# Two fused transformer blocks on one core: the first phase in another order (sums of squares in pairs, embedding chunks between the modulation chunks, stores between the loads)

## The chip, the core and the metric

One core of a Trainium2 chip runs the whole program in one launch. The metric is the device time of an execution in microseconds. 2467.18 us is the median of three runs of the kernel before (2466.94 to 2468.97). The profile is of a single further execution.

## What is computed

A residual block with adaptive modulation, a recurrent branch and latent attention, followed by a second block with sparse attention, spatial gating and a gated embedding; 512 positions, width 2048, float32. What the first phase makes is this part:

```python
def rms_norm(x, gain=None):
    xf = x.astype(jnp.float32)
    y = xf * lax.rsqrt(jnp.mean(xf * xf, axis=-1, keepdims=True) + EPS)
...
    c_act = jax.nn.silu(c)
    mod = c_act @ w_ada[l] + b_ada[l]
    shift, scale, gate = jnp.split(mod, 3, axis=-1)
    h = rms_norm(x) * (1.0 + scale[:, None, :]) + shift[:, None, :]
    proj = h @ w_in[l]
    xr, gr, qc, kvc, kr, ga = jnp.split(proj, split_points(IN_SPLITS), axis=-1)
...
        x = x + jax.nn.sigmoid(x @ w_ple_gate[l]) * (p[l] @ w_ple[l])
```

The last product, `p @ w_ple`, needs nothing but inputs. The kernel makes it in the first phase and parks it in DRAM until the end.

## The kernel before

**Weights.** All weights come as a stream of chunks of 128 x 1024 float32 (512 KB), in the order of the list `PLAN`; a chunk lies in one of twelve slots (`raw`, `rawx`) while the first phase lasts, and SyncE (SP) issues its load when the chunk twelve places before it has been used. To multiply in float32 precision, a chunk is split: ScalarE (ACT) writes the rounded upper half `whi` (L1146), GpSimd (POOL) the difference `wlo` (L2496), and TensorE (PE) does three matmuls per 128 x 128 block: `whi` with the activations' upper half (L535), `whi` with their lower half (L536), `wlo` with the upper half (L538). PE can begin with `whi` and stops at the third matmul if `wlo` is not there.

**The first phase.** The list `OPENING` sets the order of the work on PE, ACT and VectorE (DVE), each of which walks through it in its own program:

- `ple` m: one of four chunks of the embedding product, 4 blocks of 6 matmuls, 24 in all. Block n writes PSUM bank n % 6, and must wait until ACT has copied out the block that was there (L1208) into a staging tile `stg`, from where SP stores it (`pls`, L2616).
- `xsum`: the sum over the features of x squared, by matmuls with a tile of ones (L597). ACT makes the squares (L1179); then comes the root on ACT (L1221) and the reciprocal on DVE (L1860).
- `adt` e, j and `ada` e, j: chunks of the modulation weights, eight groups e of four each. DVE reduces an `adt` chunk with the silu of c in a row, `cB` (L1763), to the scales; PE multiplies an `ada` chunk with c (L613) to the shifts.
- `cols` e: the shifts' row is copied by ACT (`RW`, L1239) and turned into columns by PE (L625). DVE makes the normalised tiles `un` (L1777) and adds the shift (L1783), ACT writes their upper halves (L1187), DVE the lower ones (L1793).
- `unit` u: three matmuls of the latent projections. The first of them needs the tiles of group 0. Eight units share a chunk `wq`.

**Two chains beside it.** The silu of c in a row: for each half i, ACT takes the tanh of `cB` into `junk` (L1171), then DVE forms the product (L1753), and the second tanh waits for the first product, since `junk` is one tile. The rotary angles: 18 DVE operations on 128 x 512 tiles (L1830, L1798, L1845), then two sines on ACT (L1203).

ACT, DVE, POOL and SP each execute in program order, so what stands behind a waiting instruction waits too.

Of the kernel before, what the change touches and what calls it, by code (L numbers as in the profile page):

```python
# [12 lines left out]
P = 128  # L13
# [25 lines left out]
for _n, _w in [("ident", 128), ("ones", 128), ("bd", 128), ("perm", 128), ("t0", 512), ("t1", 512),  # L39
               ("tc", 4 * NC), ("mc", NC), ("sr", 32), ("s32", 1)]:  # L40
    CST[_n] = (_at, _at + _w)
    _at += _w
# [3 lines left out]
def opening():  # L46
# [4 lines left out]
    out = [("ple", 0), ("xsum",), ("ple", 1), ("ple", 2)]  # L51
    for e in range(8):
        u = 14 * (e - 1)
        for j in range(4):
            out.append(("adt", e, j))
            out.append(("ada", e, j))
            if e == 0 and j == 1:
                out.append(("ple", 3))
            for _ in range((0, 3, 4, 4)[j] if 0 < e < 7 else (0, 2, 2, 2)[j] if e else 0):
                out.append(("unit", u))  # L60
                u += 1
        out.append(("cols", e))
        if e:
# [101 lines left out]
def split_plan():  # L165
# [12 lines left out]
    def ahead():  # L178
        return 0 if now["use"] == 0 else 3 if now["use"] < NSTART else LOOK
# [112 lines left out]
def build(nc, wst, xt, crow, pos, vec, cst, lrw, w2bd, selb, sgw, rows, pt, x1s, tgs, pls, out):  # L292
    ctx = ExitStack()
    with ctx:
# [55 lines left out]
        stg = [at(x + 2 * i, NT, F, f"stg{x}_{i}") for x in (48, 80) for i in range(8)]  # L350
        sqx = [at(x, NT, F, f"sqx{x}") for x in (64, 66, 96, 98)]
        PF, KK, AN = at(44, NT, F, "PF"), at(46, NT, F, "KK"), [at(76, NT, F, "AN0"), at(78, NT, F, "AN1")]
# [92 lines left out]
        for n in (["vec", "cst", "pos", "selb", "lrw", "rows", "sgw", "w2bd", "pt", "x1s", "out", "plr"]  # L445
                  + [f"x{i}" for i in range(4)] + [f"raw{i}" for i in range(11 + EXTRA)]
                  + [f"ax{i}" for i in range(8)] + [f"ts{i}" for i in range(4)] + ["crow", "pls", "qsw"]
# [57 lines left out]
        def tensor(e):  # L505
# [68 lines left out]
            def embedding(m_):  # L574
                c, hi, lo = chunk("ple", m_, 0)
                w.wait_ge(*done("whi", c))
                for i in range(4):
# [11 lines left out]
                m.then_inc(*up("used_pe", "used", c))  # L589
                T.place["ple", 4 * m_ + 3] = T.place["used", c]  # L590
# [62 lines left out]
            for item in OPENING:  # L653
                if item[0] == "ple":
                    embedding(item[1])
# [474 lines left out]
        def scalar(e):  # L1130
# [43 lines left out]
            def x_squares():  # L1174
                for k in range(16):
                    w.wait_ge(f"x{k // 4}", 16)
                    if k >= 4:
                        w.wait_ge(*done("xsum", k - 4))
                    e.activation(sqx[k % 4][:, :], sub(X0, k), ACT.Square).then_inc(*up("sq_act", "xsq", k))  # L1179

            def h_uppers(g):
                if g >= 2:
                    w.wait_ge("pls", 256)
# [21 lines left out]
            def embedding(m_):  # L1205
                for n in range(4 * m_, 4 * m_ + 4):
# [4 lines left out]
            for item in OPENING:  # L1211
                if item[0] in ("ple", "adt", "ada") or item[0] == "unit" and item[1] % 8 == 0:
                    use()
                if item == ("ple", 0):
                    c_tanh(0)
                    c_tanh(1)
                    x_squares()
                elif item == ("ple", 1):
                    w.wait_ge(*done("xsum", 15))
# [3 lines left out]
                    embedding(0)  # L1223
                elif item == ("ple", 2):
                    embedding(1)
                elif item == ("adt", 0, 0):
                    embedding(2)
                    sines()
                elif item == ("adt", 0, 3):
                    embedding(3)  # L1230
                elif item[0] == "adt" and item[1] and item[2] == 0:
                    h_uppers(item[1] - 1)
# [327 lines left out]
            def attention2():  # L1560

                def tables(t):

                    a, r = PAIRS2[t]
                    if t:
                        for gb, i in PAIR_ORDER:
                            w.wait_ge(*done("smax", ("a2", t - 1, 1), gb, i))
                    for gb in range(2):
# [125 lines left out]
        def vector(e):  # L1694
# [91 lines left out]
            def h_lowers(g):  # L1786
                if g >= 2:
                    w.wait_ge("pls", 256)
# [60 lines left out]
            c_rows(0)  # L1849
            c_rows(1)  # L1850
            w.wait_ge("vec", 16)
            e.tensor_scalar(bsc, V("b_ada", 16, 16), 1.0, None, ALU.add, ALU.bypass).then_inc(*up("term_dve", "bsc"))
            angles()
            for item in OPENING:
                if item[0] == "adt":
# [5 lines left out]
                    elif g and j == 0:  # L1861
                        shifts(g - 1)
                    elif g and j == 1:
# [11 lines left out]
                elif item[0] == "cols":  # L1875
                    scaled(item[1])
            shifts(7)
# [1068 lines left out]
```

## Time and profile before

| | |
|---|---|
| median of three runs | 2467.18 us (2466.94 to 2468.97) |
| profiled execution, its own time | 2467.53 us |
| its span | 2465.8 us |
| PE busy | 2406.8 us, 98% |
| POOL, DVE, ACT busy | 984.5, 930.2, 822.7 us |
| mean granted clock of TensorE | 0.991 |
| DMA | 309.55 MB, mean 126 GB/s |

The profile names instructions by line of the kernel, tile written and tiles read. Times of start count from the beginning of the span. A row in order of time has: start, length, engine, line, operation, out<-in, form, count, and in brackets how long the engine was idle before and what ended that. An "L538 <- POOL wlo" is thus a matmul that waited for a lower half. "Granted clock" is the share of TensorE's full clock, 1.00 being 2.4 GHz.

### The profile page before, as it was taken

Reading aid. Unit: us, or ns where it says so; the run is one execution under the profiler, and the core shown is the slowest. Engines: PE = TensorE matmul, PEld = TensorE weight load, DVE = VectorE, ACT = ScalarE, POOL = GpSimd, SP = SyncE. Lnnn points to the kernel's source line nnn. Section 1 sums busy time; section 2 is a strip of 40 time slices with the busy share of each in tenths; the row PEclk is TensorE's granted clock in tenths of the full one; section 3 lists DMA queues with packets and bytes.
Section 4 is the critical chain, followed back from the end, with each engine's and each line's share of the span. In section 5 each row is a group of like instructions: output and inputs, shape, how many; then the busy total and the mean of one; then the engine's idle time right before and its main releaser. Section 6 shows DMA issues by size and latency. Waiting matters only on the chain.

```text
span 2465.8 us, 28169 instructions
## 1 busy us (share of the span) xinstructions
PE 2406.8 (98%) x11092; PEld 1906.4 (77%) x11092; DVE 930.2 (38%) x1485; ACT 822.7 (33%) x1267; POOL 984.5 (40%) x426
## 2 busy tenths in 40 slices
PE   7899999999999999999999999999999999999996
PEld 4567677778888888887887778787878888888885
DVE  4764466566500620210555534343421412202113
ACT  5245444442322332222434333333322312213321
POOL 1344333234555434443332324242434444444553
PEclk9899999999999999999999999999999999999998
DMA  8962233236444343232222323232333444454332
GB/s 294 402 245 79 60 133 108 90 107 210 150 150 135 116 161 95 88 101 87 67 86 60 93 83 107 86 109 84 108 95 102 154 146 128 131 167 121 93 103 85
DMA packets 98435, 309.55 MB, mean 126 GB/s; under 512 B 10624, under 2 KB 12032, under 8 KB 98176
## 3 DMA queue, kind: packets, MB, share of 16 engines
q1 hardware_dynamic: 98304, 307.76, 38.8%
q8 instruction: 88, 1.44, 0.3%
q14 instruction: 43, 0.35, 0.0%
HBM read 285.69 MB, written 20.97 MB: 124 GB/s over the span
## 4 chain that ended last, share of the span: by engine, by line
PE 89%; DVE 5%; ACT 2%; issue 2%; DMA 1%; SPq 1%; POOL 0%; DVEq 0%; ACTq 0%; POOLq 0%
PE bank L535 24%; PE bank L538 24%; PE bank L536 24%; PE bank L531 2%; PE bank L532 2%; PE bank L534 2%; PE bank L1030 2%; PE bank L1054 1%; PE bank L1042 1%; DVE hlo L1708 1%; DMA raw<-in_wst 1%; PE bank L829 1%; PE bank L840 1%; DVE hlo L2428 1%; DMA rawx<-in_wst 1%
## 5 line engine op out<-in xcount | busy, mean ns | idle before, releaser
L2496 POOL TENSOR_TENSOR wlo<-raw,whi 128x1024 fp32r<-128x1024 f32 x365 | 895.1, 2457 | 1248.2 <-ACT whi L1146 1240.2
L535 PE MATMUL bank<-hhi,whi 128*128 128x512 f32 x2752 | 1087.6, 395 | 19.9 <-ACT whi L1146 17.2
L538 PE MATMUL bank<-hhi,wlo 128*128 128x512 f32 x2752 | 1078.0, 392 | 7.3 <-POOL wlo L2496 7.3
L536 PE MATMUL bank<-hlo,whi 128*128 128x512 f32 x2752 | 1075.4, 391 | 0.0
L535 PEld LDWEIGHTS bank<-hhi,whi 128*128 128x128 f32 x2752 | 518.2, 188 | 144.5 <-ACT whi L1146 18.9
L538 PEld LDWEIGHTS bank<-hhi,wlo 128*128 128x128 f32 x2752 | 517.9, 188 | 123.0 <-POOL wlo L2496 13.1
L536 PEld LDWEIGHTS bank<-hlo,whi 128*128 128x128 f32 x2752 | 518.5, 188 | 106.6 <-issue 0.7
L1146 ACT ACTIVATE whi<-raw 128x1024 fp32r<-128x1024 f32 x365 | 384.5, 1055 | 594.8 <-PE bank L538 482.4
L2304 DVE TENSOR_SCALAR S<-S,sm 128x512 f32<-128x512 f32 (+1 forms) x64 | 78.0, 1218 | 0.6
L531 PE MATMUL bank<-whi,hhi 128*128 128x512 f32 x192 | 76.0, 396 | 0.0
L532 PE MATMUL bank<-whi,hlo 128*128 128x512 f32 x192 | 75.7, 394 | 0.0
L534 PE MATMUL bank<-wlo,hhi 128*128 128x512 f32 x192 | 75.6, 394 | 0.0
L1577 ACT ACTIVATE S<-S,sm 128x512 f32<-128x512 f32 (+1 forms) x64 | 35.3, 551 | 119.1 <-DVE sm L2294 119.1
L2304 DVE TENSOR_SCALAR S2b<-S2b,sm 128x512 f32<-128x512 f32 (+1 forms) x64 | 73.6, 1150 | 0.0
L2469 DVE SCALAR_TENSOR_TENSOR tgt<-tgt,MG 128x512 f32<-128x512 f32 x16 | 11.1, 693 | 141.6 <-ACT tgt L1683 141.6
L2288 DVE CUSTOM_DVE_ANT_0 S<-bank,BT 128x512 f32<-128x512 f32 (+1 forms) x64 | 31.2, 487 | 87.3 <-PE bank L1030 87.2
L2156 DVE SCALAR_TENSOR_TENSOR X<-bank,sm,axr 128x512 f32<-128x512 f32 x16 | 12.0, 750 | 137.6 <-PE bank L538 137.6
L2461 DVE TENSOR_TENSOR X<-bank,axr 128x512 f32<-128x512 f32 x16 | 11.0, 690 | 138.4 <-PE bank L538 138.4
L2320 DVE COPY PT<-bank 128x384 f32<-128x384 f32 (+2 forms) x48 | 20.0, 417 | 96.6 <-PE bank L1042 96.6
L2496 POOL TENSOR_TENSOR wlo<-rawx,whi 128x1024 fp32r<-128x1024 f32 x11 | 31.0, 2835 | 54.1 <-ACT whi L1146 41.5
L1646 ACT ACTIVATE TS<-bank 128x512 f32<-128x512 f32 x32 | 18.9, 591 | 99.9 <-PE bank L538 94.5
L1763 DVE CUSTOM_DVE_ANT_0 junk<-rawx,cB,sm 128x1024 f32<-128x1024 f32 x19 | 42.1, 2218 | 5.3 <-DMA rawx<-in_wst 4.7
(308 smaller groups left out, 2110.5 us busy)
## 6 DMA issues: line engine op xcount, KB each, us to landing
raw<-in_wst SPq DMA_DIRECT2D x397, 512.0 KB, 3.6
rawx<-in_wst SPq DMA_DIRECT2D x54, 512.0 KB, 6.8
rawy<-in_wst SPq DMA_DIRECT2D x26, 512.0 KB, 4.5
tgs<-TS SPq DMA_DIRECT2D x32, 256.0 KB, 4.0
axr<-tgs SPq DMA_DIRECT2D x32, 256.0 KB, 3.9
X<-in_xt SPq DMA_DIRECT2D x4, 1024.0 KB, 15.3
pls<-stg SPq DMA_DIRECT2D x16, 256.0 KB, 9.5
axr<-in_xt SPq DMA_DIRECT2D x16, 256.0 KB, 2.9
```

What stands on the lines that cost most here:

```text
L531: e.matmul(o, xh, hi, start=first, stop=False)
L532: e.matmul(o, xl, hi, start=False, stop=False)
L534: return e.matmul(o, xh, lo, start=False, stop=last)
L535: e.matmul(o, hi, xh, start=first, stop=False)
L536: e.matmul(o, hi, xl, start=False, stop=False)
L538: return e.matmul(o, lo, xh, start=False, stop=last)
L1030: e.matmul(bks[n][0][:, off:off + wd], qq[pb:pb + 64, P * i:P * (i + 1)], kk[pb:pb + 64, 0:wd], start=True, stop=True).then_inc(*up("score ...
L1146: e.activation(sub(whi, PAIR[c], CH), slots[slot(c)], ACT.Copy).then_inc(*up("whi_act", "whi", c))
L1577: e.activation(sl, sl, ACT.Exp, scale=SM2, bias=smx[:, 8 + k:9 + k], accum_out=smx[:, 16 + k:17 + k]).then_inc(*up("exp_act", "exp", u, gb ...
L1763: e.tensor_tensor_reduce(out=junk[:, :], in0=slots[slot(c)], in1=cB[:, 1024 * i:1024 * (i + 1)], scale=0.5, scalar=half[:, 0:1] if i else ...
L2304: e.tensor_scalar(sl, sl, ri[:, 4 * gb + i:4 * gb + i + 1], None, ALU.mult, ALU.bypass).then_inc(*up("soft_dve", "soft", u, gb, i))
L2496: e.tensor_tensor(sub(wlo, PAIR[c], CH), slots[slot(c)], sub(whi, PAIR[c], CH).bitcast(F), ALU.subtract).then_inc(*up("wlo_pool", "wlo", c))
```

## The change

`OPENING` becomes `ple 0, ple 1, xsum`, then group 0 of the modulation with `ple 2` behind its second pair and `ple 3` behind its fourth; of `ple 3` two blocks come ahead of `cols 0` and two behind it.

- Squares: sixteen tiles are squared by ACT in two portions of eight; POOL adds them by twos (eight additions, new), and PE sums eight tiles instead of sixteen. ACT does the first eight ahead of the two tanhs, the others behind the copies of blocks 0 to 3.
- DVE does the angles ahead of the two products of c, and the shift and the lower halves of group 0 at once with `cols 0`.
- SP: the constants lose one matrix (64 KB), are loaded behind x, and their two masks of 128 x 512 behind the last store. The second weight chunk and half of x come ahead of the row of c. The sixteen stores go out in four portions, between loads.
- The splits may run one chunk ahead at the very start (`ahead`).

```diff
@@ OPENING
-    out = [("ple", 0), ("xsum",), ("ple", 1), ("ple", 2)]
+    out = [("ple", 0), ("ple", 1), ("xsum",)]
...
             if e == 0 and j == 1:
-                out.append(("ple", 3))
+                out.append(("ple", 2))
...
+        if e == 0:
+            out.append(("ple", 3))
         out.append(("cols", e))
-        if e:
+        if e == 0:
+            out.append(("plelast",))
+        else:
             out.extend(("unit", v) for v in range(u, 14 * e))
@@ split_plan
-        return 0 if now["use"] == 0 else 3 if now["use"] < NSTART else LOOK
+        return 1 if now["use"] == 0 else 3 if now["use"] < NSTART else LOOK
@@ tensor
-                for k in range(16):
-                    w.wait_ge(*done("xsq", k))
-                    e.matmul(o[:, :], C("ones"), sqx[k % 4][:, :], start=k == 0, stop=k == 15).then_inc(
-                        *up("stat_pe", "xsum", k))
+                for i in range(8):
+                    w.wait_ge(*done("xpair", i))
+                    m = e.matmul(o[:, :], C("ones"), sqs[i][:, :], start=i == 0, stop=i == 7)
+                m.then_inc(*up("stat_pe", "xsum"))
@@ scalar
-            def x_squares():
-                for k in range(16):
+            def x_squares(a, b):
+                for k in range(a, b):
+                    i = k // 2
                     w.wait_ge(f"x{k // 4}", 16)
-                    if k >= 4:
-                        w.wait_ge(*done("xsum", k - 4))
-                    e.activation(sqx[k % 4][:, :], sub(X0, k), ACT.Square).then_inc(*up("sq_act", "xsq", k))
+                    if k % 2 and i >= 4:
+                        w.wait_ge(*done("xpair", i - 4))
+                    e.activation((sqt[i % 4] if k % 2 else sqs[i])[:, :], sub(X0, k), ACT.Square).then_inc(
+                        *up("sq_act", "xsq", k))
...
                 if item == ("ple", 0):
+                    x_squares(0, 8)
                     c_tanh(0)
                     c_tanh(1)
-                    x_squares()
                 elif item == ("ple", 1):
-                    w.wait_ge(*done("xsum", 15))
+                    embedding(range(4))
+                    x_squares(8, 16)
+                elif item == ("xsum",):
+                    embedding(range(4, 8))
+                    w.wait_ge(*done("xsum"))
                     w.wait_ge(*done("eps"))
                     e.activation(rsx[:, :], bank("xsum")[:, :], ACT.Sqrt, scale=1.0 / 2048, bias=epsc).then_inc(
                         *up("root_act", "xroot", frees=("xsum",)))
-                    embedding(0)
-                elif item == ("ple", 2):
-                    embedding(1)
                 elif item == ("adt", 0, 0):
-                    embedding(2)
                     sines()
-                elif item == ("adt", 0, 3):
-                    embedding(3)
+                elif item == ("adt", 0, 2):
+                    embedding(range(8, 12))
+                elif item == ("plelast",):
+                    embedding(range(12, 14))
+                    h_uppers(0)
+                    embedding(range(14, 16))
@@ vector
-            c_rows(0)
-            c_rows(1)
             w.wait_ge("vec", 16)
             e.tensor_scalar(bsc, V("b_ada", 16, 16), 1.0, None, ALU.add, ALU.bypass).then_inc(*up("term_dve", "bsc"))
             angles()
+            c_rows(0)
+            c_rows(1)
...
                 elif item[0] == "cols":
                     scaled(item[1])
+                    if item[1] == 0:
+                        shifts(0)
+                        h_lowers(0)
@@ gpsimd
-            use(NSTART)
+            use()
+            for i in range(8):
+                w.wait_ge(*done("xsq", 2 * i))
+                w.wait_ge(*done("xsq", 2 * i + 1))
+                e.tensor_tensor(sqs[i][:, :], sqs[i][:, :], sqt[i % 4][:, :], ALU.add).then_inc(
+                    *up("ssum_pool", "xpair", i))
+            use(NSTART - 1)
@@ sync
-            e.dma_start(ct[:, :], cst).then_inc(*up("cst", by=16))
             e.dma_start(PR[:, :].rearrange("p (k t) -> p k t", k=2), pt.rearrange("k p t -> p k t")).then_inc(
                 *up("pt", by=16))
-            load(0)
+            load(1)
             e.dma_start(PI32[:, :], pos.to_broadcast([P, NT])).then_inc(*up("pos", by=16))
+            x_tiles(0)
+            x_tiles(1)
             e.dma_start(cB[:, :], crow.to_broadcast([P, 2048])).then_inc(*up("crow", by=16))
-            for j in range(4):
-                x_tiles(j)
-            load(2)
-            load(INDEX["ada", 1, 1] + 12)
-            for n in range(16):
-                w.wait_ge(*done("plec", n))
-                e.dma_start(pls[n], stg[n][:, :]).then_inc(*up("pls", by=16))
+            x_tiles(2)
+            x_tiles(3)
+            first = CST["t0"][0]
+            e.dma_start(ct[:, 0:first], cst[:, 0:first]).then_inc(*up("cst", by=16))
+            load(14)
+            embedded(0)
+            embedded(1)
+            load(19)
+            embedded(2)
+            load(24)
+            embedded(3)
+            e.dma_start(ct[:, first:], cst[:, first:]).then_inc(*up("cst2", by=16))
```

`embedded(m)` stores blocks 4m to 4m + 3, each when ACT has copied it. Staging tiles and work tiles get other addresses.

What this does to the order is seen at three places. ACT between the first upper half of a weight chunk (`whi`) and the middle of the squares, before (`cB` is the row of c, `sqx` a square, `X` the input):

```order
L1146 ACTIVATE whi<-raw 128x1024
L1171 ACTIVATE junk<-cB 128x1024 x2
L1179 ACTIVATE sqx_77<-X_57 128x512
L1179 ACTIVATE sqx_78<-X_57 128x512
L1179 ACTIVATE sqx_79<-X_57 128x512
L1179 ACTIVATE sqx_80<-X_57 128x512
```

and of the change (`sqs` and `sqt` are the squares of a pair, `stg` the copies of embedding blocks):

```order
L1194 ACTIVATE sqs_80<-X_57 128x512
L1194 ACTIVATE sqt_88<-X_57 128x512
L1185 ACTIVATE junk<-cB 128x1024 x2
L1226 ACTIVATE stg_0_61<-bank 128x512
L1226 ACTIVATE stg_1_62<-bank 128x512
L1226 ACTIVATE stg_2_63<-bank 128x512
L1226 ACTIVATE stg_3_64<-bank 128x512
L1194 ACTIVATE sqs_81<-X_57 128x512
L1194 ACTIVATE sqt_85<-X_57 128x512
```

The tanhs (`junk`) have moved behind eight squares, and four copies and the other eight squares stand behind the tanhs.

DVE from the lower halves of the embedding's input to the first angle operations, before:

```order
L1723 TENSOR_TENSOR hlo<-PR,hhi 128x512 x2
L1753 SCALAR_TENSOR_TENSOR cB<-junk,cB 128x1024 x2
L1852 TENSOR_SCALAR sm<-vt 128x16
L1830 CAST PF<-PI_95 128x512
L1798 TENSOR_SCALAR PF<-PF,vt 128x512
L1798 TENSOR_SCALAR KK<-PF 128x512
```

and of the change, the end of the angles (`KK`, `AN`) and the first reduction of a modulation chunk (`raw`):

```order
L1824 TENSOR_SCALAR KK<-PF 128x512
L1824 TENSOR_SCALAR KK<-KK 128x512 x2
L1871 SCALAR_TENSOR_TENSOR AN_92<-KK,PF 128x512
L1871 SCALAR_TENSOR_TENSOR AN_92<-KK,AN_92 128x512 x2
L1824 TENSOR_SCALAR AN_92<-AN_92 128x512 x2
L1777 SCALAR_TENSOR_TENSOR cB<-junk,cB 128x1024 x2
L1787 ISA junk,sm<-raw,cB,sm 128x1024
```

The two products of c have moved from ahead of the first angle operation to behind the last one.

POOL at the start of the change; before, only the `wlo` rows stood there:

```order
L2526 TENSOR_TENSOR wlo<-raw,whi 128x1024 x2
L2545 TENSOR_TENSOR sqs_77<-sqs_77,sqt_85 128x512
L2545 TENSOR_TENSOR sqs_78<-sqs_78,sqt_86 128x512
L2545 TENSOR_TENSOR sqs_79<-sqs_79,sqt_87 128x512
L2545 TENSOR_TENSOR sqs_80<-sqs_80,sqt_88 128x512
L2545 TENSOR_TENSOR sqs_81<-sqs_81,sqt_85 128x512
L2545 TENSOR_TENSOR sqs_82<-sqs_82,sqt_86 128x512
L2545 TENSOR_TENSOR sqs_83<-sqs_83,sqt_87 128x512
L2545 TENSOR_TENSOR sqs_84<-sqs_84,sqt_88 128x512
L2526 TENSOR_TENSOR wlo<-rawx_106,whi 128x1024
```

The lower halves of the first two chunks come directly one after the other, and that of the third only behind all eight additions.

## Rows read from the trace of the kernel before

**Rows 1.** The page, busy time, share of the span, instructions of each engine

```profile
PE 2406.8 (98%) x11092; PEld 1906.4 (77%) x11092; DVE 930.2 (38%) x1485; ACT 822.7 (33%) x1267; POOL 984.5 (40%) x426
```

**Rows 2.** By stretch: busy PE, PEld, DVE, ACT, POOL, then clock, DMA share, GB/s

```profile
0.00:20.00 20.00, 8.16 (x25) 6.06 (x26) 6.29 (x14) 7.91 (x11) 2.55 (x5) 1.00 0.91 321
...
40.00:60.00 20.00, 15.22 (x75) 10.90 (x77) 4.74 (x7) 8.23 (x13) 2.35 (x1) 0.83 0.51 176
...
180.00:2465.80 2285.80, 2252.62 (x10329) 1803.72 (x10327) 816.82 (x1336) 750.18 (x1160) 930.13 (x402) 0.99 0.36 110
```

**Rows 3.** Waits of PE, 0 to 180 us: total, times, longest

```profile
PE bank L535 <- ACT whi L1146: 17.2, 4, 10.6
PE bank L538 <- POOL wlo L2496: 7.3, 6, 1.7
```

**Rows 4.** PE in order of time, 0 to 100 us

```profile
19.73 13.89 PE L597 MATMUL bank<-sqx,ct 128*128 128x512 f32 x32
...
51.59 0.79 PE L538 MATMUL bank<-hhi,wlo 128*128 128x512 f32 x1 [1.69 <-POOL wlo L2496]
...
57.30 0.41 PE L535 MATMUL bank<-hhi,whi 128*128 128x512 f32 x1
...
59.49 1.07 PE L613 MATMUL bank<-rawx,c 128*32 128x256 f32 x16
...
68.35 0.79 PE L538 MATMUL bank<-hhi,wlo 128*128 128x512 f32 x1 [1.22 <-POOL wlo L2496]
...
88.13 0.79 PE L538 MATMUL bank<-hhi,wlo 128*128 128x512 f32 x1 [1.69 <-POOL wlo L2496]
...
91.32 0.46 PE L535 MATMUL bank<-hhi,whi 128*128 128x512 f32 x1
```

**Rows 5.** ACT in order of time, 0 to 50 us

```profile
15.90 1.06 ACT L1171 ACTIVATE junk<-cB 128x1024 f32<-128x1024 f32 x1 [1.29 <-DVE cB L1753]
16.86 2.18 ACT L1179 ACTIVATE sqx<-X 128x512 f32<-128x512 f32 x4
...
32.77 1.28 ACT L1221 ACT_TABLE_LOAD   x1
34.07 0.69 ACT L1221 ACTIVATE rsx<-bank,sm 128x512 f32<-128x512 f32 x1
34.65 3.03 ACT L1208 ACTIVATE stg<-bank 128x512 f32<-128x512 f32 x6
```

**Rows 6.** DVE in order of time, 0 to 110 us

```profile
18.21 0.42 DVE L1830 CAST PF<-PI 128x512 f32<-128x512 int32 x1
...
27.23 0.89 DVE L1798 TENSOR_SCALAR AN<-AN 128x512 f32<-128x512 f32 x2
28.23 1.28 DVE L1763 CUSTOM_DVE_ANT_0 junk<-raw,cB,sm 128x1024 f32<-128x1024 f32 x1
...
34.63 3.11 DVE L1763 CUSTOM_DVE_ANT_0 junk<-rawx,cB,sm 128x1024 f32<-128x1024 f32 x1 [2.55 <-DMA rawx<-in_wst]
...
37.67 3.34 DVE L1860 RECIPROCAL rsx<-rsx 128x512 f32<-128x512 f32 x1
...
100.16 3.47 DVE L1763 CUSTOM_DVE_ANT_0 junk<-raw,cB,sm 128x1024 f32<-128x1024 f32 x1
```

**Rows 7.** POOL in order of time, POOL by group, and DVE on a softmax tile

```profile
10.66 2.35 POOL L2496 TENSOR_TENSOR wlo<-raw,whi 128x1024 fp32r<-128x1024 f32 x1 [10.14 <-ACT whi L1146]
31.89 4.76 POOL L2496 TENSOR_TENSOR wlo<-raw,whi 128x1024 fp32r<-128x1024 f32 x2 [18.88 <-ACT whi L1146]
...
102.54 3.35 POOL L2496 TENSOR_TENSOR wlo<-rawx,whi 128x1024 fp32r<-128x1024 f32 x1
...
L2537 POOL TENSOR_TENSOR ssb<-ssb,sqb 128x512 f32<-128x512 f32 x14 | 18.0, 1287 | 45.5 <-ACT sqb L1480 45.5
...
L2304 DVE TENSOR_SCALAR S2b<-S2b,sm x64: 271/481/2561, 1182.8 to 1816.6; 128x512 f32<-128x512 f32 x16, 128x384 f32<-128x384 f32 x16, 128x256 f32<-128x256 f32 x16, 128x128 f32<-128x128 f32 x16
```

**Rows 8.** DMA issues, 0 to 40 us: count, KB each, us to landing

```profile
ct<-in_cst SPq DMA_DIRECT2D x1, 862.0 KB, 5.7
```

More of the change, by code:

```diff
@@ L38 @@
 _at = 0
-for _n, _w in [("ident", 128), ("ones", 128), ("bd", 128), ("perm", 128), ("t0", 512), ("t1", 512),
-               ("tc", 4 * NC), ("mc", NC), ("sr", 32), ("s32", 1)]:
+for _n, _w in [("ident", 128), ("ones", 128), ("perm", 128), ("tc", 4 * NC), ("mc", NC), ("sr", 32),
+               ("s32", 1), ("t0", 512), ("t1", 512)]:
     CST[_n] = (_at, _at + _w)
@@ L349, in build @@
         cB = area(34, 1, "cB", F, 2048)
[L350 to L352 removed]
+        stg = [at(x + 2 * i, NT, F, f"stg{x}_{i}") for x in (48, 80, 56, 88) for i in range(4)]
+        sqs = [at(x, NT, F, f"sqs{x}") for x in (40, 42, 44, 46, 72, 74, 76, 78)]
+        sqt = [at(x, NT, F, f"sqt{x}") for x in (64, 66, 96, 98)]
+        PF, KK, AN = area(42, 1, "PF"), area(44, 1, "KK"), [area(46, 1, "AN0"), area(107, 1, "AN1")]
         rsx = area(48, 1, "rsx")
@@ L446, in build @@
                   + [f"x{i}" for i in range(4)] + [f"raw{i}" for i in range(11 + EXTRA)]
-                  + [f"ax{i}" for i in range(8)] + [f"ts{i}" for i in range(4)] + ["crow", "pls", "qsw"]
+                  + [f"ax{i}" for i in range(8)] + [f"ts{i}" for i in range(4)] + ["crow", "plsa", "plsb", "cst2", "qsw"]
                   + ["used_pe", "adac_pe", "proj_pe", "stat_pe", "rot_pe", "tok_pe", "score_pe", "tr_pe", "pv_pe",
@@ L571, in led, with embedding @@
                                       h == 0, h == 1, o[:, :], prior, (name, n))
-            def embedding(m_):
-                c, hi, lo = chunk("ple", m_, 0)
+            def embedding(m_, part):
+                if 0 in part:
+                    ple["c"] = chunk("ple", m_, 0)
+                c, hi, lo = ple["c"]
                 w.wait_ge(*done("whi", c))
-                for i in range(4):
+                for i in part:
                     n = 4 * m_ + i
@@ L588, in embedding @@
                         m.then_inc(*up("ple_pe", "ple", n))
-                m.then_inc(*up("used_pe", "used", c))
-                T.place["ple", 4 * m_ + 3] = T.place["used", c]
+                    else:
+                        m.then_inc(*up("used_pe", "used", c))
+                        T.place["ple", n] = T.place["used", c]
+            ple = {}
             def x_sum():
@@ L654, in tensor @@
                 if item[0] == "ple":
-                    embedding(item[1])
+                    embedding(item[1], range(4) if item[1] < 3 else range(2))
+                elif item[0] == "plelast":
+                    embedding(3, range(2, 4))
                 elif item[0] == "xsum":
@@ L1203, in sines, with embedding @@
                     e.activation(dst[:, :], AN[n][:, :], ACT.Sin).then_inc(*up("term_act", "trig", n))
-            def embedding(m_):
-                for n in range(4 * m_, 4 * m_ + 4):
+            def embedding(blocks):
+                for n in blocks:
                     w.wait_ge(*done("ple", n))
```

25 lines of the change are left out of this document (18 added, 7 removed).

## The prediction

> **What bounds the kernel now.** I read the busy line of the page first, then busy time by stretch, then TensorE (PE) in order of time, then the engines that feed it. PE is busy 98% of the span [rows 1], and from 180 us to the end it is busy 2252.6 of 2285.8 us [rows 2]: there only its own work counts, so a change in the first phase is worth exactly what it moves the moment at which PE has its backlog. Before that moment PE is not full: 15.2 us of 20 between 40 and 60 us, with a granted clock of 0.83 [rows 2]. What it waits for are never transfers: the longest total is for the rounded upper halves of weights, which ScalarE (ACT) makes [rows 3], and then for the lower halves, which GpSimd (POOL) makes. The place to compare is the first product of the latent projections (unit 0): its third matmul starts at 68.35 us [rows 4]. Behind it units, modulation rows and columns follow in the same order in both kernels, and I let them take the same time.
>
> The DMA queue stands still for about half of 40 to 60 us (share 0.51 [rows 2]). The new order of loads and stores fills some of that hole. I cost this at nothing, because no wait of PE before 180 us ends with a transfer; the cover is the lead that the loads have, and a rival below prices its loss.
>
> **The sum.** I walk the new order with the old durations. All times are of one profiled execution: 2467.53 us, 2465.8 of it span; the median of the runs shown is 2467.18.
>
> 1. *Constants out of the way.* 862 KB stood ahead of the first weights [rows 8]; at the 321 GB/s of the first 20 us [rows 2] that is up to 2.7 us; I take 2.3, a little less, as the first transfers also wait for their issue. ACT's first upper half and POOL's lower half behind it move by that, the latter from 10.66 to 8.35, done at 10.7 [rows 7]. The second follows directly. PE does embedding chunk 0 until 17.4 and two blocks of chunk 1 until 20.1.
>
> 2. *VectorE (DVE) now does the angles first, and ACT waits behind them.* Blocks 6 and 7 write the banks of blocks 0 and 1, which ACT must first empty. ACT's copies stand behind the tanh of the second half of c, and that waits for DVE's product of the first half (the old row shows this wait, 1.29 us [rows 5]). That product now stands behind 18 angle operations, 18.21 to 28.12 in the old trace, 9.9 us [rows 6].
>
> 3. *POOL works at the same time, and the two exclude each other.* A reduction of 1.28 us (28.23) took 3.11 when it began 2.02 us before POOL was done (34.63 against 31.89 + 4.76): it was extended by 1.83, 0.91 of the overlap [rows 6, 7]. The other way about, POOL's 2.35 became 3.35 while a DVE operation ended [rows 6, 7]: they take turns. In the old kernel POOL did nothing during the angles. Now one lower half (2.35) and the first four additions (1.29 each, the nearest row being the same operation on another tile [rows 7]) fall among them: 7.5 us. Of this I take off 1.5 us: a blocked operation loses a little less than the whole wait (1.83 of 2.02, so 0.19, on DVE; 3.35 instead of 1.09 + 2.35, so 0.09, on POOL), and there are six of the one and five of the other. From the end of the first lower half: 10.7 + 9.9 + 7.5 - 1.5 = 26.6 us. The Trainium skill ("SBUF — State Buffer", Reading the diagram) says that the loser fully blocks. By that the 1.5 us are not saved here nor later, and the sum would be about 1.4 us larger.
>
> 4. *The sum of squares.* DVE's product (1.2) ends at 27.8, the tanh (1.06 [rows 5]) at 28.9, the first copy at 29.5, the fourth at 31.0 (six in 3.03 [rows 5]), the last eight squares at 35.4 (four in 2.18 [rows 5]). POOL's last four additions run from 32.7 to 38.9, one reduction of 1.28 between them. PE has been idle for 9.4 us; its two blocks take 2.9 at half clock, to 32.4. A sum matmul took 13.89 / 16 = 0.87 us at full clock [rows 4]. Eight, two of them at half clock, end at 40.9. So halving the matmuls takes 6.9 us of PE work away, and the sum still ends 7 us later than the old 33.6, but with chunk 1 behind it.
>
> 5. *Chunk 2.* The table load is not held by the wait (it ran at 32.77, before the sum was done [rows 5]); root 0.69, table 1.28, two sines 1.2, upper half 1.04: 45.0 us. POOL finds DVE in a reduction (the reciprocal, 3.34 [rows 6], ends at 44.9) and is done at 48.4. Chunk 3 of the old kernel resumed at 51.59 and ended at 59.49 [rows 4], 7.9 us; so chunk 2 ends at 56.3, two modulation rows at 57.4.
>
> 6. *Chunk 3 in two halves.* Its upper half now waits for ACT's copies of chunk 2: 57.9, the lower half 60.3. Ten matmuls resume there. At full clock one takes 0.23 to 0.24 (nine from 57.30 to 59.49), at half twice that; the restart at 88.13 was slow for 3.2 us [rows 4], so the ten take 3.9: 64.2. Columns about 0.5, the last half chunk 12 x 0.23 = 2.7, two modulation rows 1.1 [rows 4]: 68.5. The row copy, the shift and the first normalised tiles are covered by these halves; this removes the old idle time before 61 us.
>
> 7. *Unit 0.* ACT: copy to 67.9, small terms 1.7 (a table load of 1.28 and two short operations), upper half at 70.7; POOL with half a turn of waiting, 73.5 us. Against 68.35 that is **+5.2 us**: 2467.5 + 5.2 - 0.35 (profiled run to median) = **2472.4 us**.
>
> The parts with one answer: 64 KB of a constant dropped and 512 KB of masks loaded after the stores move transfers, which PE does not wait for; the masks are used in the attention, long after the first phase. Eight additions on an idle POOL cost PE nothing but through the turns above. The bounds: if no operation of DVE were extended, below; if all turns are full, +6.6.
>
> **Rivals.** (a) *The two engines don't collide on the angles*, half of whose operations have one input, where the operation that was extended has two. Against it: a one-input scaling of a softmax tile has a longest case of 2561 ns over a median of 481 [rows 7]. Then the angles end near 19.5, the copies start at 21.8, the x tiles become the limit, the sum ends at 30.5, and chunk 2 resumes at 37 to 38 instead of 48.4. The rest of the walk is the same: unit 0 at 62.8, -5.5 us, 2461.7. It decides wherever DVE's first product of c is done before about 24 us.
>
> (b) *The slow-clock stretches shrink.* After the restart at 51.59 matmuls were slow until 57.30, 5.7 us, after that at 88.13 only 3.2 us [rows 4], and a slow microsecond costs (7.9 - 24 x 0.23) / 5.7 = 0.42. If the restarts at 48.4 and 73.5 come out as the short ones, and one more vanishes with the filled holes, 2.1 to 3.2 us come back: 2469.8, no change that can be told. For it: PE stands still for a shorter time ahead of unit 0 than before.
>
> (c) *The synchronisation queue.* Loads behind the last stores can't issue before ACT's last copy at 67.9, and load 24 waits for a reduction on DVE at 69. With a transfer of 1.3 us each, the next weights that ACT wants (some 16 us after unit 0) land near 80. That leaves about 10 us; once it is used up, each late microsecond is PE's. With 5 us beyond: 2478. Against it: the old queue was later than this and PE waited for no transfer.
>
> **How the numbers follow.** A difference of 0.2% (4.9 us) is about what a measurement of this kernel can tell. The walk gets 0.55; +5.2 lies close to that line, but what I left out (full turns, a later first copy) mostly adds, so 0.4 of it is beyond the line and 0.15 within it. Case (b) 0.19, (a) 0.18, (c) and full turns 0.08. So slower 0.48, same 0.34, faster 0.18. The range takes in (a) and (c): 2461.5 to 2478.
>
> **What the new profile would show.** Right: the angle operations stretched to about 1.5 us each from 10 to 20 us, the product of c ending near 28, PE idle from 20 to 29, the sum ending near 41, unit 0 past 72. Wrong: PE's blocks 6 and 7 start before 24 us, or the groups behind unit 0 run at another pace than 13 us each, or PE waits for a transfer.

## The result, and the profile after

The changed kernel takes 2471.88 us (median of 16 runs, 2470.54 to 2475.34), the kernel before 2468.7 us (16 runs, 2465.6 to 2470.28). The ratio is 1.0017, 95% interval 1.001 to 1.0024: 3 to 4 us longer. The prediction was 2472.4. The profiled execution has a span of 2469.4 us, against 2465.8 before.

Busy time, the counterpart of [rows 1], and by stretch, of [rows 2]:

```profile
PE 2403.5 (97%) x11076; PEld 1904.9 (77%) x11076; DVE 934.6 (38%) x1485; ACT 821.0 (33%) x1267; POOL 999.7 (40%) x434
```

```profile
20.00:40.00 20.00, 12.50 (x33) 7.33 (x31) 12.45 (x18) 10.38 (x18) 7.32 (x5) 0.74 1.03 406
40.00:60.00 20.00, 12.50 (x60) 7.59 (x58) 7.83 (x5) 7.67 (x11) 5.53 (x2) 0.74 0.82 301
60.00:80.00 20.00, 15.99 (x69) 10.72 (x70) 13.77 (x16) 7.11 (x11) 5.25 (x3) 0.74 0.75 274
```

The hole in the transfers between 40 and 60 us is largely filled (301 GB/s instead of 176), and PE does less there than before: 12.5 us busy instead of 15.22. Its clock is 0.74 in three stretches in a row. Waits of PE up to 180 us (total, times, longest), to be held against [rows 3]:

```profile
PE bank L541 <- ACT whi L1160: 14.3, 5, 7.7
PE bank L544 <- POOL wlo L2526: 10.0, 6, 2.1
PE bank L541 <- ACT stg L1226: 7.5, 1, 7.5
```

The wait for an upper half is 2.9 us shorter in sum, that for a lower half 2.7 longer, and a new one of 7.5 us stands beside them. PE in order of time, as [rows 4]:

```profile
28.50 0.79 PE L541 MATMUL bank<-hhi,whi 128*128 128x512 f32 x1 [7.50 <-ACT stg L1226]
...
33.33 0.39 PE L544 MATMUL bank<-hhi,wlo 128*128 128x512 f32 x1
33.56 7.03 PE L609 MATMUL bank<-sqs,ct 128*128 128x512 f32 x16
...
48.06 0.79 PE L544 MATMUL bank<-hhi,wlo 128*128 128x512 f32 x1 [2.07 <-POOL wlo L2526]
...
55.95 1.07 PE L625 MATMUL bank<-rawx,c 128*32 128x256 f32 x16
...
60.08 0.50 PE L544 MATMUL bank<-hhi,wlo 128*128 128x512 f32 x1 [1.70 <-POOL wlo L2526]
...
73.47 0.79 PE L544 MATMUL bank<-hhi,wlo 128*128 128x512 f32 x1 [1.68 <-POOL wlo L2526]
...
77.73 0.50 PE L541 MATMUL bank<-hhi,whi 128*128 128x512 f32 x1
...
92.80 0.51 PE L544 MATMUL bank<-hhi,wlo 128*128 128x512 f32 x1 [2.12 <-POOL wlo L2526]
...
102.81 1.07 PE L625 MATMUL bank<-rawx,c 128*32 128x256 f32 x16
```

The new wait is the first row: block 6 can't be written until ACT has copied block 0. Why ACT is late there, its own rows tell ([rows 5] before):

```profile
26.90 1.06 ACT L1185 ACTIVATE junk<-cB 128x1024 f32<-128x1024 f32 x1 [8.00 <-DVE cB L1777]
27.87 2.04 ACT L1226 ACTIVATE stg<-bank 128x512 f32<-128x512 f32 x4
...
40.62 0.69 ACT L1243 ACTIVATE rsx<-bank,sm 128x512 f32<-128x512 f32 x1 [3.32 <-PE bank L609]
```

ACT does nothing for 8 us with four finished blocks behind it, because the second tanh writes the tile that DVE's first product still has to read. DVE is in the angles until 25.7 us ([rows 6] before), and six of its 18 operations, those that meet POOL's work, take two to five times as long as before (`PF<-PF,vt` 2.47 us instead of 0.49, the pair of `AN<-KK,AN` 3.38 instead of 1.42, the pair of `AN<-AN` 1.86 instead of 0.89); the others keep their times ([rows 7] before):

```profile
9.94 0.43 DVE L1856 CAST PF<-PI 128x512 f32<-128x512 int32 x1 [2.60 <-DMA PI<-in_pos]
10.40 2.47 DVE L1824 TENSOR_SCALAR PF<-PF,vt 128x512 f32<-128x512 f32 x1
...
15.97 3.38 DVE L1871 SCALAR_TENSOR_TENSOR AN<-KK,AN 128x512 f32<-128x512 f32 x2
19.39 1.86 DVE L1824 TENSOR_SCALAR AN<-AN 128x512 f32<-128x512 f32 x2
...
25.65 1.22 DVE L1777 SCALAR_TENSOR_TENSOR cB<-junk,cB 128x1024 f32<-128x1024 f32 x1
```

```profile
7.71 4.88 POOL L2526 TENSOR_TENSOR wlo<-raw,whi 128x1024 fp32r<-128x1024 f32 x2 [7.20 <-ACT whi L1160]
13.91 6.59 POOL L2545 TENSOR_TENSOR sqs<-sqs,sqt 128x512 f32<-128x512 f32 x4 [1.32 <-ACT sqt L1194]
31.08 6.82 POOL L2545 TENSOR_TENSOR sqs<-sqs,sqt 128x512 f32<-128x512 f32 x4 [10.58 <-ACT sqt L1194]
```

Unit 0's third matmul comes at 73.47 us, 5.12 later than before. Of this, part is back by the first row of group 3: 102.81 against 99.60, 3.2 us. Between these two marks PE's work is the same; the restart near 90 us differs. Before, it ran at the lower clock for 3.2 us (88.13 to 91.32), with a first matmul of 0.79 us; after, the same matmul takes 0.51. From that restart to the row of group 3 it was 11.47 us and is 10.01 now (1.46 less), from unit 0 to that restart 19.78 and now 19.33 (0.45 less). Behind group 3 nothing more is gained: group 7 begins at 156.48 instead of 153.25, 3.2 us later, which is the 3.2 us between the medians.

### The profile page after: what moved, and what is told of

It is laid out like the page before. It is cut to its first block, busy times and chain, and to the rows that moved or that the text cites. A ratio compares the mean times of both kernels' runs of the same rounds, so it can differ in the third digit from the quotient of the medians.

```text
span 2469.4 us, 28155 instructions
## 1 busy us (share of the span) xinstructions
PE 2403.5 (97%) x11076; PEld 1904.9 (77%) x11076; DVE 934.6 (38%) x1485; ACT 821.0 (33%) x1267; POOL 999.7 (40%) x434
## 4 chain that ended last, share of the span: by engine, by line
PE 88%; DVE 5%; issue 3%; ACT 2%; DMA 1%; POOL 1%; SPq 0%; DVEq 0%; ACTq 0%; POOLq 0%
PE bank L541 24%; PE bank L544 24%; PE bank L542 24%; PE bank L537 2%; PE bank L538 2%; PE bank L540 2%; PE bank L1044 2%; PE bank L1068 1%; PE bank L1056 1%; DVE hlo L1732 1%; PE bank L843 1%; PE bank L854 1%; DVE hlo L2458 1%; PE bank L884 1%; DMA raw<-in_wst 0%
## 5 line engine op out<-in xcount | busy, mean ns | idle before, releaser
L2600 POOL TENSOR_TENSOR ssc<-ssc,sqc 128x512 f32<-128x512 f32 x14 | 18.1, 1295 | 62.3 <-ACT sqc L1712 62.3
```

## The experiments

Kernels timed together share the runs of the kernel before on the same chip, and each ratio is to those. Where a kernel's own median is set against the changed kernel, 2471.88 is meant. As a mark of progress I give the moment at which the first row of group 7 starts (156.5 us in the change, 153.2 before); from there to the end the order of the work is the same in all of them. The expected texts count the runs in the order in which they were made: their first run is section 1, their third section 3, their fifth ("the first of this call") the first kernel of section 8, their ninth the last kernel of section 8.

### 1. Products of c ahead of the angles

```diff
-            angles()
             c_rows(0)
             c_rows(1)
+            angles()
```

> One part of the change undone: VectorE makes the two products of c ahead of the 18 angle operations again; all else as changed. My theory (copies of blocks 0 to 3 stand behind the second tanh, that behind the product, that behind the angles): second tanh near 20 us instead of 26.9, PE's stop at block 6 shrinks from 7.5 us to about 1, sum of squares done near 32 instead of 40.5. The sines then wait for the angles, so chunk 2 resumes near 42 instead of 48.06, and unit 0's third matmul comes near 67 instead of 73.5: 6 us less than the change, 2 to 3 us less than before (2466). Rival 'the additional stops at chunks 2 and 3 are the loss, the early part doesn't matter': chunk 2 resumes above 46, time within 2 us of the change. Rival 'order of the transfers': no difference at all.

2464.87 us, ratio 0.9988 (0.9979 to 0.9997). The rows of ACT and PE:

```profile
20.03 1.06 ACT L1185 ACTIVATE junk<-cB 128x1024 f32<-128x1024 f32 x1 [1.38 <-DVE cB L1777]
...
36.02 0.63 ACT L1221 ACTIVATE COS<-AN 128x512 f32<-128x512 f32 x1 [1.42 <-DVE AN L1824]
```

```profile
21.63 0.50 PE L541 MATMUL bank<-hhi,whi 128*128 128x512 f32 x1 [1.91 <-ACT stg L1226]
24.52 7.41 PE L609 MATMUL bank<-sqs,ct 128*128 128x512 f32 x16
...
37.65 0.79 PE L541 MATMUL bank<-hhi,whi 128*128 128x512 f32 x1 [4.71 <-ACT whi L1160]
```

The tanh comes 6.9 us earlier, the sum of squares ends at 31.9 instead of 40.6, and group 7 begins at 149.2. Putting two DVE instructions back where they were takes 7 us off, so this place is where the change loses. It doesn't hand on all 8.7 us of the sum: chunk 2 now waits 4.71 us for its upper half, as the root and the sines stand between, and the second sine itself waits 1.42 us for the angles, which DVE now ends later.

### 2. The eight additions left out

This kernel leaves the additions on POOL out, so the sum of squares covers only the even one of each pair of tiles; all else is as in the change.

```diff
-                e.tensor_tensor(sqs[i][:, :], sqs[i][:, :], sqt[i % 4][:, :], ALU.add)...
+                T.place["xpair", i] = done("xsq", 2 * i + 1)
```

> The eight additions on GpSimd are left out (the sum of squares then covers only the even tiles); all else as changed. Price of the turns between GpSimd and VectorE: if they exclude each other as the prediction has it, the angles end near 22 us instead of 25.7, the second tanh starts at 23 instead of 26.9, the sum is done near 35.5 instead of 40.5, and the time is 4 to 5 us less than that of the change. If they only share bandwidth or don't meet, the angles still end near 25.7 and the time stays within 1 us.

2466.9 us, ratio 1.0001 (0.9992 to 1.001): 5 us less than the change by the medians, 4 by the ratios, as expected. DVE:

```profile
15.14 1.42 DVE L1871 SCALAR_TENSOR_TENSOR AN<-KK,AN 128x512 f32<-128x512 f32 x2
16.60 0.89 DVE L1824 TENSOR_SCALAR AN<-AN 128x512 f32<-128x512 f32 x2
...
21.89 1.22 DVE L1777 SCALAR_TENSOR_TENSOR cB<-junk,cB 128x1024 f32<-128x1024 f32 x1
```

The same pairs of operations took 3.38 and 1.86 with the additions beside them. The product of c comes at 21.89 instead of 25.65, so the additions lengthen the angles by 3.8 us. PE's stop at block 6 is 5.1 us instead of 7.5, the sum ends at 37.2 (35.5 expected), and group 7 begins at 153.4. The collision is real and is the smaller part of the delay; the larger is the place of the product (run 1 has the additions and wins more).

### 3. Splits one chunk further ahead

```diff
-        return 1 if now["use"] == 0 else 3 if now["use"] < NSTART else LOOK
+        return 1 if now["use"] == 0 else 4 if now["use"] < NSTART else LOOK
```

> As changed, but weights may be split four items ahead of their use in the first phase instead of three: upper halves of chunks 2 and 3 then stand ahead of the sines and ahead of the copies of chunk 2. My theory of the later stops (each chunk's upper half queued behind ScalarE work that waits for PE): chunk 2 resumes near 45 instead of 48.06, the stops of 0.6 and 1.7 us at chunk 3 and its slow restart go, unit 0's third matmul near 64 instead of 73.5, time 8 to 10 us less than the change, some 5 us less than before (2463). Rival 'the loss is all in the first 40 us and PE catches up behind it anyway because transfers limit': less than 3 us gained.

2453.78 us (five runs, 2453.47 to 2460.12), ratio 0.9949 (0.9937 to 0.9962): 18 us faster than the change by the medians, 17 by the ratios, with the late tanh still in it. ACT and PE:

```profile
40.48 1.05 ACT L1160 ACTIVATE whi<-rawx 128x1024 fp32r<-128x1024 f32 x1
...
43.89 1.05 ACT L1160 ACTIVATE whi<-rawx 128x1024 fp32r<-128x1024 f32 x1
```

```profile
41.57 0.50 PE L541 MATMUL bank<-hhi,whi 128*128 128x512 f32 x1 [0.72 <-ACT whi L1160]
...
44.01 0.50 PE L544 MATMUL bank<-hhi,wlo 128*128 128x512 f32 x1 [1.71 <-POOL wlo L2526]
```

The upper half of chunk 2 no longer stands behind the table load and the sines. The stops at chunk 3 are gone, and so are the slow restarts behind them: the clock granted from 40 to 60 us is 1.00 (0.74 in the change), and group 7 begins at 139.0. The stops that the walk carried over from the old kernel as given (upper halves that ACT makes too late) cost more than the late tanh: taking them away is worth 17 to 18 us, taking the tanh's delay away 7.

### 4. The same in the kernel before

> The kernel before the change with the one number of the third run: splits four items ahead. If the distance of the splits is what the changed order makes good use of (its embedding chunks stand between modulation chunks, where three items ahead is too late), the kernel before gains less than the change did: the stops at 49 to 51.6 and at 86 to 88 us go, that at 66 mostly stays, 2456 to 2460, and the changed order with the same number (2453.8) is the faster one. If the distance helps both alike, it gains 18 us: 2449.

2457.87 us, ratio 0.9956 (0.9944 to 0.9969), 10.6 us faster than before. The old order gains 10.6 from the same number that gives the new order 17 to 18, so the new order is no longer the slower one. That it is the faster one is likely but not shown: its median is 4 us lower and its group 7 begins at 139.0 instead of 141.9, but the two ratios are 0.9949 and 0.9956, and their intervals overlap. What the old one still has is a wait for DVE, and one of 1.99 us for a transfer at 77.4:

```profile
57.70 0.77 PE L535 MATMUL bank<-hhi,whi 128*128 128x512 f32 x1 [3.02 <-DVE hlo L1793]
```

### 5. The angles first, in the kernel before

The edit of run 1 the other way about: `c_rows(0)` and `c_rows(1)` behind `angles()`, with nothing else of the change.

> One part of the change alone, put into the kernel before: VectorE makes the angles ahead of the products of c. GpSimd does nothing there, so the angles take their 9.9 us, from 11 to 21. By my theory the second tanh starts near 22.4 instead of 15.9, all squares stand behind it, the sum of squares ends near 40 instead of 33.6 and all behind it is 6 us later: 2472 to 2474. Rival 'the order of these two matters only through the collision with GpSimd': within 2 us of before.

2477.59 us, ratio 1.0036 (1.0022 to 1.005), 9 us slower than before, more than expected. ACT:

```profile
23.27 1.06 ACT L1171 ACTIVATE junk<-cB 128x1024 f32<-128x1024 f32 x1 [9.38 <-DVE cB L1753]
```

In the old order all sixteen squares stand behind this tanh; PE stops for 5.8 us at 25.0 and the sum ends at 41.1 instead of 33.6. Alone, this part of the change costs 9 us; the rest of the change (halved sum, chunks between, loads earlier) brings about 5 of them back.

### 6. A second tile for the tanh

The tanh of the second half gets a tile of its own, so it needs no product; ACT waits for the second product only ahead of `plelast`.

```diff
+        junk2 = at(88, 1024, F, "junkb")
...
-                if i:
-                    w.wait_ge(*done("cB", i - 1))
-                e.activation(junk[:, :], cB[...
+                e.activation((junk2 if i else junk)[:, :], cB[...
```

> The change with nothing but the tile of its own for the second tanh. ScalarE's wait behind the angles is the first-run loss without moving any VectorE work: PE's stop of 7.5 us at block 6 goes, the sum is done near 30 to 31 us instead of 40.6, and the time is as good as that of the first run or better: 2462 to 2465, against 2471.9 for the change and 2467 to 2468 before. Rival 'VectorE itself is the limit there, the wait of ScalarE only shows it': within 2 us of the change.

2463.68 us, ratio 0.9981 (0.9972 to 0.999). PE:

```profile
20.60 0.50 PE L542 MATMUL bank<-hhi,whi 128*128 128x512 f32 x1 [0.86 <-ACT stg L1225]
...
24.25 7.13 PE L610 MATMUL bank<-sqs,ct 128*128 128x512 f32 x16 [0.60 <-DMA ct<-in_cst]
```

The angles stay first and the additions stay, and the stop shrinks from 7.5 to 0.86 us. It was the wait on ACT that cost, not DVE's order in itself.

### 7. The stores in one portion

```diff
-            load(14)
-            embedded(0)
-            embedded(1)
-            load(19)
-            embedded(2)
             load(24)
+            embedded(0)
+            embedded(1)
+            embedded(2)
             embedded(3)
```

> As changed, but the sixteen stores of the embedding stand together behind load 24, as before the change, instead of between loads 14, 19 and 24. My theory (PE waits for no transfer here): same time within 1 us, the loads of 15 to 24 a few us earlier, those behind them later. Rival 'the stores between the loads are what costs (or what gives back) the time': over 2 us either way.

2479.75 us, ratio 1.0048 (1.0034 to 1.0062), 8 us slower than the change. I had expected no difference, and that theory falls. SP of the change, then of this kernel:

```profile
68.74 2.26 SPq L2643 DMA_DIRECT2D pls<-stg  x4
...
72.18 1.64 SPq L2633 DMA_DIRECT2D raw<-in_wst  x3
```

```profile
69.22 11.30 SPq L2643 DMA_DIRECT2D pls<-stg  x16
...
81.25 1.77 SPq L2633 DMA_DIRECT2D raw<-in_wst  x3
```

Sixteen issues take 11.3 us, and load 25 and the next ones go out 9 us later. PE pays for it at 93 us:

```profile
93.08 0.50 PE L541 MATMUL bank<-hhi,whi 128*128 128x512 f32 x1 [2.91 <-ACT whi L1160]
...
96.56 0.80 PE L544 MATMUL bank<-hhi,wlo 128*128 128x512 f32 x1 [2.75 <-POOL wlo L2526]
```

PE's list of waits names ACT and POOL. Their own rows show what lies behind. Ahead of the first stop ACT stands 3.77 us, until 91.87, for a small term of DVE, and DVE's reduction ahead of that term waits for a transfer; the same reduction ran at 87.32 in the change, without a wait:

```profile
90.46 1.28 DVE L1787 CUSTOM_DVE_ANT_0 junk<-raw,cB,sm 128x1024 f32<-128x1024 f32 x1 [2.50 <-DMA raw<-in_wst]
```

Ahead of the second, ACT's upper half at 95.58 us waited 2.55 us for the transfer of `rawx`. After these stops PE runs at the lower clock until about 102, which it didn't in the change. Group 7 begins at 162.8 us, 6.3 later than in the change; the rest of the 8 us lies behind it. The lead of the loads, which I had counted as cover, is about as long as the block of stores. The transfers also lose time before: from 40 to 60 us, where the change moves 301 GB/s, this kernel moves 155.

### 8. Runs 1 and 3 together, and two attempts behind it

> The change with both edits: products of c ahead of the angles, and splits four items ahead. If the two losses are separate, they add: 7 us (first run) and 18 us (third run) off the change, 2447. But in the third run a weight chunk was split the moment it landed (landed 69.42 us, split 69.45), so the transfers are next in line: by that theory the gain stops half way, at 2449 to 2451, with waits on transfers in front of the upper halves between 50 and 80 us.

2459.33 us, ratio 0.9963 (0.9951 to 0.9975): not better than run 3 alone. The sum of squares ends at 32.3 instead of 39.9, but group 7 begins at 142.4 instead of 139.0. SP's waits up to 60 us, and PE:

```profile
SPq L2633 <- DVE sm L1787: 16.3, 3, 14.7
```

```profile
76.62 0.77 PE L541 MATMUL bank<-hhi,whi 128*128 128x512 f32 x1 [4.77 <-DVE hlo L1819]
```

With the products first DVE stands idle for 11.8 us, until 19.0, waiting for the first tanh, and only then come the angles and behind them its first reductions, at 38.2 us (29.4 in the change). These free the slots of load 14 and the ones behind it; load 14 is now issued at 39.6 us, 8.9 later than in run 3; the lost time of the queue, then busy at 360 to 369 GB/s from 20 to 60 us (392 to 406 in run 3), is not made up. Then an upper half that ACT is to make ahead of its work for group 2 waits for a transfer (72.44 us, after 8.15 of waiting), and what stands behind it waits too.

Next, the same kernel with the splits five ahead from use 7 on (counted from 0):

> As the first of this call, with splits five items ahead from item 7 on: the first chunk of the latent projections (unit 0) is then split ahead of the copies of the last half embedding chunk and of a table load on ScalarE. The stop ahead of unit 0 (0.6 and 2.2 us in the third run) goes if the chunk has landed by then: 2 to 3 us less than without. If transfers are the limit by now: the same time.

2459.5 us, ratio 0.9966 (0.9954 to 0.9979), a miss. ACT:

```profile
52.08 1.06 ACT L1160 ACTIVATE whi<-rawx 128x1024 fp32r<-128x1024 f32 x1 [7.26 <-DMA rawx<-in_wst]
53.04 0.37 ACT L1262 ACTIVATE RW<-bank 128x256 f32<-128x256 f32 x1
```

The row copy that PE waits for (5.29 us, at 53.46) had been ready to go; it stood behind an upper half whose chunk had not landed. A split too far ahead holds up what stands behind it: five ahead gained nothing over four here.

And run 6 with run 3, where both the tanh and the loads are early:

> As the third run (splits four items ahead), and the second tanh writes a tile of its own, so that ScalarE no longer waits for VectorE's product; VectorE keeps the order of the change (angles first). By my theory of the fifth run (there the reductions of the modulation chunks came behind the angles, slot 2 came free late and load 14 was issued at 39.6 us instead of 30.7, and the transfers ran late): this version takes PE's stop at block 6 away without moving the angles. Copies of blocks 0 to 3 near 20 us, sum done near 30 to 31 instead of 39.9, chunk 2 resumes near 35 instead of 44, load 14 still issued by 32. Time 4 to 8 us below the third run's 2453.8, less than the 9 us won early because transfers come next. Rival: it ends at 2457 or more like the fifth run, and then the early start itself costs, not the late load.

2455.53 us, ratio 0.9948 (0.9935 to 0.996), no better than run 3. The sum ends at 31.2, and from 20 to 80 us the transfers run at 406, 410 and 412 GB/s, about the most that any stretch of 20 us here shows (413, in the next section). ACT:

```profile
69.18 1.06 ACT L1161 ACTIVATE whi<-raw 128x1024 fp32r<-128x1024 f32 x1 [6.83 <-DMA raw<-in_wst]
70.14 1.32 ACT L1204 ACTIVATE hhi<-un,sm 128x512 fp32r<-128x512 f32 x2
```

PE waits 4.78 us at 73.35 for the lower halves `hlo` that come from this `hhi`. The 8.7 us won at the sum are gone by then: the weights land no sooner.

### 9. The activations' upper halves ahead of the splits

The last kernel of section 8 with two more edits: `h_uppers` ahead of the splits for groups from 1 on, and the masks' transfer behind more loads.

```diff
+                if item[0] == "adt" and item[1] > 1 and item[2] == 0:
+                    h_uppers(item[1] - 1)
                 if item[0] in ("ple", "adt", "ada") or ...:
                     use()
...
-            e.dma_start(ct[:, first:], cst[:, first:]).then_inc(*up("cst2", by=16))
             load(INDEX["win1", 24, 1] + 6)
+            e.dma_start(ct[:, first:], cst[:, first:]).then_inc(*up("cst2", by=16))
```

> As the ninth run (own tile for the second tanh, splits four items ahead), with ScalarE making the upper halves of a group's tiles ahead of the split that waits for a transfer, and the two masks loaded behind the first phase's last chunks. In the ninth run the transfers were full from 20 to 80 us, and PE stood 4.8 us at 73.4 for tiles whose upper halves stood behind a split that waited for its chunk (landed 69.16). By my theory that stop shrinks to about 2 us, and the transfers end 1.3 us earlier: 2451 to 2453, 3 us below the ninth run and level with or just under the third (2453.8). If the transfers alone set the pace whatever the order: only the 1.3 us of the masks, 2454.

2449.79 us (five runs, 2448.76 to 2451.97), ratio 0.9927 (0.9914 to 0.994): the best of all, 22 us faster than the change. ACT and busy time by stretch:

```profile
65.08 1.34 ACT L1204 ACTIVATE hhi<-un,sm 128x512 fp32r<-128x512 f32 x2 [3.16 <-DVE sm L1807]
67.15 1.06 ACT L1161 ACTIVATE whi<-raw 128x1024 fp32r<-128x1024 f32 x1 [0.73 <-DMA raw<-in_wst]
```

```profile
60.00:80.00 20.00, 19.31 (x113) 13.33 (x112) 16.95 (x23) 6.79 (x10) 6.94 (x3) 1.00 1.03 413
```

`hhi` now comes at 65.08 instead of 70.14, the stop of 4.78 us is gone (the longest between 60 and 90 us is 0.69), and group 7 begins at 134.3. The chunk that ACT waited for also landed 2 us earlier (its split starts at 67.15 instead of 69.18). What each of the two edits is worth is not separated.

The same two edits without the second tile:

> The same two edits without the tile of its own, so on the third run, in which no tile waited this way (its wait at 61 us is for POOL): upper halves first change nothing there, the masks at most 1.3 us: 2452.5 to 2454. If it is clearly below the run with the own tile, starting early is of no use once the transfers are full; level with it if both sit on the same limit.

2458.61 us (2454.02 to 2460.78), ratio 0.9952 (0.9938 to 0.9966), a miss. Its interval lies on that of run 3, to which it adds the two edits. Two of its five times, 2454.02 and 2454.52, are where the expected text has them, and the profiled execution was the longest of the five. That the edits help where ACT waits for a landing is shown by the pair with the second tile (group 7 at 139.6 without them and 134.3 with them); in this kernel no gain was seen, and why its group 7 begins 3.8 us later than that of run 3 stays open (1.0 of it is there at the end of the sum already).

## Why the prediction was right

By its own steps, with what the profile after shows:

1. *Constants.* Lower half at 8.35 said, 7.71 measured.
2. *ACT behind the angles.* As said. Run 6 shows that it is the shared tile, run 5 that this alone costs 9 us in the old order.
3. *The turns.* Said: angles until 26.6, an extension of 6.0 us. Measured: 25.7, 15.7 us from the start instead of 9.9, so 5.8. Without the additions 3.8 of it is gone. The 6.0 came from 7.5 us of POOL's work less 1.5 for six and five small savings, and six operations were indeed extended. A one-input operation is blocked as well (2.47 us here, 0.49 in run 1, where POOL stands still beside it), which speaks against rival (a). The Trainium skill ("SBUF — State Buffer", Reading the diagram) says that the loser fully blocks; the sum would then have given 7.5 us. The trace agrees that the engines take turns, but the total is a quarter less than full blocking makes it.
4. *Sum of squares.* 40.9 said, 40.6 measured; PE's idle time 9.4 said, 7.5 measured: it stopped at 21.0 instead of 20.1, and block 6 started at 28.5 instead of 29.5. That the end fits so well is luck. The two blocks are twelve matmuls, and 2.9 us is what they take at full clock, not at half: they took 5.1, nearly all of it at the lower clock, to 33.6 instead of 32.4. The sum then ran at full clock throughout, 7.0 us, where the walk gave it 8.5. With the earlier start this made up for the slip.
5. *Chunk 2.* Resumes at 48.4 said, 48.06 measured; its rows at 56.3 said, 55.95 measured.
6. *Chunk 3.* 60.3 said, 60.08 measured; columns at 64.2, measured 64.06.
7. *Unit 0.* 73.5 said, 73.47 measured: +5.1 us.

What failed lies behind the last step: "Behind it units, modulation rows and columns follow in the same order in both kernels, and I let them take the same time." They took 1.9 us less, 1.46 of it through the mechanism of rival (b), a restart at the lower clock that vanished. That is less than the 2.1 to 3.2 us given there, and the rest of (b) came about only in part: after 48.06 the lower clock held until 53.77, 5.7 us, as long as the walk had it, and after 73.47 until 77.7, 4.3 us. So +3.2 and not +5.2. The ratio of 1.0017 therefore lies within the 0.2% line, where I had put less than on the side beyond it; the walk's distance to that line, 0.3 us, was smaller than this one term. The time itself, 2472.4 said and 2471.88 measured, fits better than the difference does, and that is luck as well: the difference was 2.0 us too large, and the three runs behind the 2467.18 lay 1.5 us under the median of sixteen, 2468.7.

Steps 5 to 7 took the stops at chunk 2, chunk 3 and unit 0 over from the old order unquestioned. Run 3 shows that a single number moves them, by more than three times the predicted effect. What the change is worth hangs on that number: with 4 instead of 3, the new order is level with the old one or a little faster (runs 3 and 4).

Rival (c) did not come about, but its mechanism is real. "I cost this at nothing, because no wait of PE before 180 us ends with a transfer" was right as a result and thin as a reason. Run 7 shows that nine more microseconds in the queue are not covered: 8 of them reach the end, and PE's list of waits still names no transfer.

## What to carry to other kernels

When an engine's order is changed, ask for each instruction moved back who waits for it and what is queued behind that waiter: here two 1.2 us products behind the angles stopped four copies, eight squares and PE for 7.5 us, and a second tile for the tanh removed the stop. A wait for a split made on another engine says that this engine was late, not why: look in its queue for the table load, the transfer or the square that stood ahead, and try how far ahead the split may go in both directions (3 was too late, 5 gained nothing over 4 and showed a new wait). Stores behind the loads on one queue are free only as long as the loads' lead lasts, which an experiment with the stores in one block measures.

## What the runs showed that I had not expected

- Restarts after a stop of the same kind and length are not alike: after 1.69 us at 88.13 (before) the lower clock of 1.2 GHz held for 3.2 us, after 2.12 us at 92.80 (after) the engine came back at 2.4 GHz at once.
- Two engines that take turns share the loss: the four additions of 1.29 us took 6.59 together (1.4 more), while DVE lost 3.8.
- Sixteen store issues take 11.3 us on SP in run 7, 0.7 each. Whether the issues or the bytes set this pace was not tested: the 16 transfers are 4.2 MB, and from 69 to 81 us the DMA engines were busy for a share of 0.97, at 336 GB/s, by which 4.2 MB alone take an estimated 12.5 us.
- The time from the first row of group 7 to the end of the span differs between executions of the same work by more than 3 us (2312.9 in the profiled ones of the change and of run 3, 2316.1 in that of run 2), which is why a difference of a few microseconds needed many runs, and why the rows up to 180 us were the better measure.
